# Expert outputs added into a DRAM table of x2 by accumulating scatters, last gate/up weights in two halves, PSUM banks dealt out anew

## What is computed

```python
h2 = _rmsnorm(x, norm2_g) * (1.0 + sc2) + sh2
out = 0
for e in range(32):                      # combine is 0 but for the 2 experts of a token
    hid = silu(h2 @ e_gate[e]) * (h2 @ e_up[e])
    out = out + combine[:, e:e + 1] * (hid @ e_down[e])
x = x + gt2 * out
return _rmsnorm(x, final_norm_g)
```

## Time and profile before

| | |
|---|---|
| median of 3 runs | 1564.2 us (1562.95 to 1564.62) |
| profiled execution, its own time | 1561.74 us |
| its span | 1560.0 us |
| PE busy | 1366.2 us, 88% |
| DVE busy | 598.3 us, 38% |
| ACT busy | 452.2 us, 29% |
| POOL busy | 239.4 us, 15% |
| DMA | 322.78 MB, mean 207 GB/s |
| mean granted PE clock | 0.945 of full speed |

### The profile page before, as it was taken

How to read it: one execution, slowest core, us unless ns; L and a number is a source line. 1 busy time by engine, 2 the same in 40 slices (tenths; PEclk the granted TensorE clock), 3 DMA queues, 4 the chain that set the end, 5 groups by cost and what they waited for, 6 DMA issues and landing times. The chain is left out here.

```text
span 1560.0 us, 30399 instructions
## 1 busy us (share of the span) xinstructions
PE 1366.2 (88%) x13439; PEld 1005.8 (64%) x13439; DVE 598.3 (38%) x1045; ACT 452.2 (29%) x724; POOL 239.4 (15%) x248
## 2 busy tenths in 40 slices
PE   4999999999999996888878999979987888788875
PEld 1788998888998996777767998763333333233322
DVE  3222234452225445555635567542221222112116
ACT  3333243344554543333334543211000000000002
POOL 3000100000112113233400202001111111111116
PEclk9999999999999997999989999969999999999988
DMA  9466442222432120000032264089999999999995
GB/s 335 159 203 206 146 157 68 68 83 89 141 103 68 55 55 23 5 4 4 7 127 68 83 214 155 34 347 403 424 428 426 428 426 427 426 428 426 426 403 197
DMA packets 128554, 322.78 MB, mean 207 GB/s; under 512 B 13849, under 2 KB 99059, under 8 KB 112514
## 3 DMA queue, kind: packets, MB, share of 16 engines
q1 hardware_dynamic: 114224, 289.27, 48.6%
q10 hardware_dynamic: 7522, 15.57, 2.9%
q0 software_dynamic: 6672, 15.95, 2.8%
HBM read 303.25 MB, written 25.11 MB: 210 GB/s over the span
## 5 line engine op out<-in xcount | busy, mean ns | idle before, releaser
L798 PE MATMUL bank<-upper_r 128*128 128x272 f32 x3168 | 419.7, 291 | 5.4 <-DVE upper_r L1037 5.4
L798 PEld LDWEIGHTS bank<-upper_r 128*128 128x128 f32 x3168 | 403.0, 189 | 30.1 <-issue 29.1
L2657 PE MATMUL bank<-upper7b,lower 128*64 128x512 f32 x912 | 254.9, 656 | 74.4 <-issue 73.6
L2657 PEld LDWEIGHTS bank<-upper7b,lower 128*64 128x64 f32 x912 | 84.3, 151 | 208.3 <-issue 206.7
L1014 DVE TENSOR_TENSOR upper_r<-upper,upper_r 128x1024 fp32r<-128x1024 f32 x66 | 82.8, 1255 | 292.5 <-ACT upper_r L571 292.3
L2464 ACT ACTIVATE lower<-bank 128x256 f32<-128x256 f32 x32 | 12.3, 384 | 438.2 <-PE bank L2666 438.2
L3011 DVE COPY lower<-bank 128x512 f32<-128x512 f32 x32 | 22.1, 692 | 278.4 <-PE bank L2657 278.4
L2520 PE MATMUL bank<-upper_r 128*128 128x272 f32 x768 | 103.0, 294 | 2.7 <-DVE upper_r L2906 2.7
L2520 PEld LDWEIGHTS bank<-upper_r 128*128 128x128 f32 x768 | 99.4, 191 | 5.4 <-DVE upper_r L2738 3.1
L2679 PE MATMUL bank<-upper7b,lower 128*64 128x512 f32 x432 | 98.4, 596 | 0.0
L2269 POOL DMA_INDIRECT expert_out<-lower x30 | 44.5, 1484 | 220.8 <-DVE lower L3034 217.2
(11 more groups left out here) (399 smaller groups left out, 1824.0 us busy)
## 6 DMA issues: line engine op xcount, KB each, us to landing
upper7b<-in_expert_w_gate SPq DMA_DIRECT2D x29, 2048.0 KB, 31.3
upper7b<-in_expert_w_up SPq DMA_DIRECT2D x28, 2048.0 KB, 32.9
upper7b<-in_expert_w_down SPq DMA_DIRECT2D x27, 2048.0 KB, 27.9
upper<-in_w_in SPq DMA_DIRECT2D x66, 512.0 KB, 3.8
lower<-in_w_ada SPq DMA_DIRECT2D x23, 1024.0 KB, 5.0
lower<-in_expert_w_down SPq DMA_DIRECT2D x5, 2048.0 KB, 30.0
lower<-in_expert_w_up SPq DMA_DIRECT2D x4, 2048.0 KB, 36.7
lower<-in_expert_w_gate SPq DMA_DIRECT2D x3, 2048.0 KB, 30.7
```

Of the source, the lines that this page charges most:

```text
L798: m = mm(psum[s][:, c, 0:HALF], w_part[s][:, k, :], h_part[:, k, c * HALF:(c + 1) * HALF], start=k == 0 and w_part is w_high and h_part is ...
L2657: m = nc.tensor.matmul(psum[s][64 * b:64 * b + 64, 1, :], x_t[(e // 2) % 2][:, k, s * BLK:(s + 1) * BLK], w[:, k, :], start=k == 0, stop=k ...
```

## The change

1. The table `expert_out` (4T half rows) becomes `expert_sum` (2T half rows, one per token and half). It is not cleared; it starts as x2. The clearing, its row of zeros and the waits for it go.
2. ACT, after each store of h2, also stores that tile of x2 into the table: five more DMAs on its queue.
3. The scatters add to the table (`compute_op=ALU.add`). Since two experts may add to one token's row, scatter e waits on POOL until scatter e-1 has landed, and scatter 0 until x2 is stored.
4. At the end SP reads five tiles of the table into x2 itself. POOL's sums, DVE's `summed`, and POOL's and ACT's share of the final product go; DVE makes all five tiles' outputs. The norm row `fin_g` is loaded ahead of the waits for the scatters instead of behind the reads.
5. Gate and up of expert 31 are loaded as the first half of gate, the first half of up, then the second half of each. PE waits for the second halves before its fifth k.
6. gate/up, turned hidden rows and down get other PSUM banks, and `last_down` for expert 30 runs ahead of down(31) for two tiles instead of one.

```diff
@@ head of the program
-        ys_dram = scratch("expert_out", (T * 4, D // 2))
+        sum_dram = scratch("expert_sum", (T * 2, D // 2))
...
-                pool.dma_start(ys_dram.rearrange("(p n) d -> p n d", p=P),
-                               zero_row[:, 0:512].unsqueeze(1).broadcast_to([P, 17, 512])).then_inc(ys_zero, 16)
...
-                        if g < 2:
-                            act.wait_ge(ys_zero, 16)
-                        else:
+                        if g >= 2:
@@ banks and loads
+        def gu_bank(s):
+            return psum[2 * s][:, 1 - s, :]
+        def hid_bank(s):
+            return psum[1 + s][:, 1, :]
+        def dn_bank(s):
+            return psum[3][:, s, :]
...
+            if kind == "down" or e < NE - 1:
+                sp.dma_start(weights_of(kind, e), source[e]).then_inc(landed[e % 3], 16)
+            else:
+                sp.dma_start(weights_of(kind, e)[:, 0:4], source[e][:, 0:4]).then_inc(landed[e % 3], 16)
+
+        def load_last_half(sp):
+            for kind, source in (("gate", egate), ("up", eup)):
+                sp.dma_start(weights_of(kind, NE - 1)[:, 4:8], source[NE - 1][:, 4:8]).then_inc(wg_rest_in, 16)
@@ SP
                         load_unit(sp, n)
+                        if STREAM[n] == ("up", NE - 1):
+                            load_last_half(sp)
                     sp.wait_ge(gu_mm, r * NE + (NE - 1))
                     sp.sem_inc(held, 1)
-                    sp.wait_ge(dn_mm, r * NE + (NE - 2))
-                    sp.sem_inc(held, 1)
+                    sp.dma_start(fin_g, I["final_norm_g"].partition_broadcast(P)).then_inc(last_rows_in, 16)
                     for s in range(2):
                         sp.wait_ge(y_out9[s], r * (16 * Y_USES[s]) + 16 * Y_USES[s])
                         sp.sem_inc(held, 1)
                     for j, n in TILES:
-                        sp.dma_start(gath[j][0:n].rearrange("t k d -> t (k d)"), ys_v[j * P:j * P + n]
-                                     ).then_inc(gathered[j], 16)
-                    sp.dma_start(fin_g, I["final_norm_g"].partition_broadcast(P)).then_inc(last_rows_in, 16)
+                        sp.dma_start(x2[0:n, j, :], sum_v[j * P:j * P + n]).then_inc(x3_in[j], 16)
@@ POOL
                 def scatter(r, e):
                     pool.wait_ge(y_done, r * NE + (e + 1))
                     pool.sem_inc(held, 1)
-                    pool.indirect_dma_start(ys_dram,
+                    if e:
+                        t = (e - 1) % 2
+                        pool.wait_ge(y_out9[t], r * (16 * Y_USES[t]) + 16 * ((e - 1) // 2 + 1))
+                    else:
+                        pool.wait_ge(x2_kept, r * 80 + 80)
+                    pool.sem_inc(held, 1)
+                    pool.indirect_dma_start(sum_dram,
                                             bass.IndirectOffsetOnAxis(ap=as_u32(y_idx[:, e:e + 1]), axis=0),
-                                            y_blk[e % 2], None, bounds_check=NY - 1, oob_is_err=False
-                                            ).then_inc(y_out9[e % 2], 16)
+                                            y_blk[e % 2], None, bounds_check=NY - 1, oob_is_err=False,
+                                            compute_op=ALU.add).then_inc(y_out9[e % 2], 16)
...
-                    for j, n in TILES:
-                        g = gath[j]
-                        pool.wait_ge(gathered[j], r * 16 + 16)
-                        pool.sem_inc(held, 1)
-                        pool.tensor_tensor(g[0:n, 0, :], g[0:n, 0, :], g[0:n, 1, :], ALU.add).then_inc(g_sum, 1)
...
-                        pool.tensor_tensor(x_fin[j], x2s[i], fin_g, ALU.mult).then_inc(f_pool, 1)
@@ ACT
                     act.dma_start(h2_dram[j * P:j * P + n], h2[i % 2][0:n]).then_inc(h2_kept[i % 2], 16)
+                    act.dma_start(sum_v[j * P:j * P + n], x2[0:n, j, :]).then_inc(x2_kept, 16)
...
-                            nc.scalar.activation(x2s[j - 1], x2[:, j - 1, :], ACT.Copy, scale=sums2[:, j - 1:j]
-                                                 ).then_inc(f_scaled, 1)
@@ PE
                     for k in range(KD):
+                        if e == NE - 1 and k == 4:
+                            pe.wait_ge(wg_rest_in, r * 32 + 32)
+                            pe.sem_inc(held, 1)
...
                         if e == NE - 1:
-                            last_down(r, 0, 0)
+                            for j in range(2):
+                                last_down(r, j, 0)
                         down(r, e)
...
-                    last_down(r, 0, 1)
-                    for j in range(1, 5):
+                    for j in range(2):
+                        last_down(r, j, 1)
+                    for j in range(2, 5):
                         for i in range(NL):
                             last_down(r, j, i)
@@ DVE
-                def summed(r, j):
-                    v.wait_ge(g_sum, r * 6 + (j + 1))
-                    ve.tensor_tensor(x2[:, j, :], x2[:, j, :], gath[j][:, 0, :], ALU.add).then_inc(x2_sum, 1)
...
+                    v.wait_ge(x3_in[j], r * 16 + 16)
...
-                    ve.reciprocal(rs, rs).then_inc(f_done, 1)
-                    if j not in BY_POOL:
-                        v.wait_ge(f_done, r * 8 + NORM_AT[j][0])
-                        ve.scalar_tensor_tensor(out=x_fin[j][0:n], in0=x2[0:n, j, :], scalar=rs, in1=fin_g[0:n],
-                                                op0=ALU.mult, op1=ALU.mult).then_inc(f_done, 1)
+                    ve.reciprocal(rs, rs).then_inc(f_rs, 1)
+                    v.wait_ge(f_rs, r * 5 + (j + 1))
+                    ve.scalar_tensor_tensor(out=x_fin[j][0:n], in0=x2[0:n, j, :], scalar=rs, in1=fin_g[0:n],
+                                            op0=ALU.mult, op1=ALU.mult).then_inc(f_done, 1)
...
+                    for j in range(2):
+                        last_added(r, j)
+                    for j in range(5):
+                        normed(r, j)
+                        if j + 2 < 5:
+                            last_added(r, j + 2)
```

More of the change, by code:

```diff
@@ L184, in build @@
         stage = [S2.take(T) for _ in range(2)]
-        zero_row = Region(chunk_at + R_WORDS + 2 * KD * P).take(D)
         z_at = S2.at
@@ L310, in build @@
         zeroed = sem("zeroed")
-        ys_zero = sem("ys_zero")
         xa_in = sem("xa_in")
@@ L444, in _ @@
                 pool.sem_inc(consts_done, 1)
-                step(pool.memset(zero_row, 0.0))
                 step(pool.memset(alpha_up[0:33, :], 0.0))
@@ L1847, in build @@
         RT_ROWS = RT_CONST + 2 + 24
-        NY = 4 * T
+        NY = 2 * T
         ORDER = [TILES[0], TILES[4], TILES[1], TILES[2], TILES[3]]
@@ L1952, in weights_of @@
             return Region(unit_at(kind, e)).take(*((4, D) if kind == "down" else (KD, FF)))
[L1953 to L1956, removed]
+        fin_g = Region(unit_at("up", NE - 2)).take(D)
+        x_fin = [Region(unit_at("down", NE - 3) + j * D).take(D) for j in range(4)]
+        x_fin.append(Region(unit_at("up", NE - 2) + D).take(D))
         fin_junk = Region(unit_at("gate", NE - 1)).take(D)
@@ L1967, in load_unit @@
             source, landed = {"gate": (egate, wg_in), "up": (eup, wg_in), "down": (edown, wd_in)}[kind]
-            sp.dma_start(weights_of(kind, e), source[e]).then_inc(landed[e % 3], 16)
+            if kind == "down" or e < NE - 1:
[5 more added lines that the diff above has]
+                sp.dma_start(weights_of(kind, NE - 1)[:, 4:8], source[NE - 1][:, 4:8]).then_inc(wg_rest_in, 16)
+        wg_rest_in = sem("wg_rest_in")
+        x2_kept = sem("x2_kept")
         yr_free = sem("yr_free")
@@ L2089, in build @@
         last_mm = sem("last_mm")
-        gathered = [sem(f"gathered{j}") for j, _ in TILES]
-        g_sum = sem("g_sum")
-        x2_sum = sem("x2_sum")
+        x3_in = [sem(f"x3_in{j}") for j, _ in TILES]
         x3_done = sem("x3_done")
@@ L2095, in build @@
         f_std = sem("f_std")
+        f_rs = sem("f_rs")
         f_done = sem("f_done")
-        f_scaled = sem("f_scaled")
-        f_pool = sem("f_pool")
         y_final = sem("y_final")
@@ L2105, in build @@
         Y_USES = [len(range(s, E_LAST, 2)) for s in range(2)]
[L2107 to L2110, removed]
+        sum_v = sum_dram.rearrange("(t b) c -> t (b c)", b=2)
         def first(r):
@@ L2164, in a_round @@
                         sp.sem_inc(held, 1)
-                        sp.wait_ge(blk_zero, r * 1 + 1)
-                        sp.sem_inc(held, 1)
-                        sp.dma_start(ys_dram.rearrange("(p n) d -> p n d", p=P),
-                                     zero_half.unsqueeze(1).broadcast_to([P, 17, 512])).then_inc(y_cleared, 16)
+                        for j, n in TILES:
+                            sp.dma_start(sum_v[j * P:j * P + n], x2[0:n, j, :]).then_inc(x2_kept, 16)
                         for n in range(8):
@@ L2184, in a_round @@
                     for j, n in TILES:
```

(13 more changed lines are left out.)

49 lines of the change are left out of this document (7 added, 42 removed).

## The result

The changed kernel has a median of 1567.88 us (1562.59 to 1575.33, 16 runs) against 1562.11 us of the kernel before (1557.67 to 1564.62, 16 runs). The ratio is 1.0041, with a 95% interval of 1.0028 to 1.0054: slower by 0.4%, on the forecast's side and a little short of its size (+7.9 us, 0.5%; 1567.9 where 1572 was forecast). The profiled execution has a span of 1566.3 us (1560.0 before) and took 1568.12 us.

A forecast was written before the change was run, and what follows sets the result against it. The prediction took the DMA engines to bound the expert stage until the last weights land. Its terms, -7.6 (end) + 1.2 (x2 store) + 14.3 (adding scatters) = +7.9 us, gave 1572 us; range 1555 to 1588, the forecast's own 1567 to 1578.

The forecast's parts named there:

- The stage is bound by the DMA engines: Expert stage: DMA engines, busy all the time at 427 GB/s, set the pace until the last weights land.
- The added row is charged like a read: Adding scatters: fetching destination rows costs as much again as POOL's rows do now, 11.0 us on the mean engine.
- the dearer rival: Adding scatters: the add costs the engine two further reads' worth, +14.3 us more, 1586 us; chance 0.13.
- The slow engines carry 1.3 times the mean: Weight stream: uneven POOL rows, from a lag of some 6 us beside 24 us, raise the add's 11.0 to 14.3 us.
- The x2 store: ACT's queue: one of five stores falls into the weight stream and costs 1.2 us, bounds 0 to 5.
- The wait for the landing costs nothing: POOL in the expert loop: scatter e waiting for scatter e-1 costs 0; later scatters only shift up to some 15 us.
- rival two: Serial scatters become the bound if landing exceeds 15.6 us per expert; at 17.8 it costs 64 us, 1636; chance 0.07.
- The end: After the weights: earlier last matmuls and no POOL sums in DVE's way shorten it by 7.6 us, bounds -7.6 to -4.
- the rival of the idle halves: Last gate and up load: first and second halves land together, so the tail gives only 4.1 us, 1575.6; chance 0.04.
- PE's waits: Profile sign in the expert stage: PE's waits before gate/up grow by some 14 us in all.
- Clearing and its cover: Early in the run: removing the clearing of expert_out is worth 0; without PE's cover its DMA costs at most 15.3 us.
- the free read: Adding scatters: the engine reads and writes at once, add costs 0, queue share stays 4.9%, 1557.8 us; chance 0.32.

The follow-up runs named there:

- add_and_wait: The kernel before with scatters that add into its own cleared table, each also waiting on POOL until the previous one has landed: 1574.14 us, ratio 1.0097.
- add_alone: The kernel before with only its scatters adding into its own cleared table, none waiting for another: 1572.84 us against 1559.73, ratio 1.0084.
- even_before: The kernel before with each expert's few used slots spread over more partitions instead of the block's front: 1552.28 us against 1556.72, ratio 0.9973.
- no_halves: The changed kernel without the split load of the last gate and up weights: 1569.21 us, ratio to the kernel before 1.0082.
- sums_on_pe: The kernel before with split last weights, new PSUM banks, and the two choices summed by PE through identity matmuls instead of by POOL: ratio 1.0031.

## Why the prediction was right, and where it was off

**The stage is bound by the DMA engines.** Right: the loss is in the stream, and no wait on POOL or PE made it (add_and_wait).

**The added row is charged like a read.** Right in kind, and sized too low: the mean engine pays some 13 us (22.5 to 36.0 us from 1040 to 1540), against 11.0 forecast. The packet records of POOL's queue in the two traces show what it pays for. In the kernel before, 2094 are of 4096 bytes; 1088 of them are gathered rows, and 1006 carry two scattered rows each, some 160 ns. Another 32 carry one scattered row (2052 bytes, 85 ns). That makes 10.2 us of 16 engines for the scattered rows. In the changed kernel the same 2044 rows are 2044 records of 2048 bytes and 176 ns, 22.5 us: 2.2 times. Smaller packets, the dearer rival's reason, are the least of it, since a plain row by itself takes 85 ns and not 80; the other 91 ns lie near the 80 that half a gathered row, the same size, takes. The Trainium skill (Collectives: The Full Stack, The bandwidth ceiling: the fold count and why AG ≠ RS ≠ AR) has a collective's reduce in the DMA path at half the speed of a copy for its two source reads. This trace agrees on the price, 176 against 80 to 85 ns for a row; the reads themselves it doesn't count.

**The slow engines carry 1.3 times the mean.** The product of 14.3 us was good (13.7 in add_alone), its factors were not, and that is luck in part. The mean charge came out 2 us higher than forecast, and the stream with the old slots grew by about that mean charge (13.7 us in add_alone), not by 1.3 times it. By the prediction's own step, lag over POOL's time in the stage, the 4.1 us of even_before would give 4.1 / 24 = 0.17 and a factor of 1.17. What the runs do show is the direction: with even slots the same charge of 13.0 us lengthened the stream by only 10.5. Why it is less than the charge stays open.

**The x2 store**: 1.2 forecast, 1.3 by ACT's queue, 1.0 by the stream. The sum for the stream was 15.5, and 15.2 came.

**The wait for the landing costs nothing.** Right (520.3 against 520.4 us), and landings of 10.8 to 12.8 us lie in the forecast span of 10 to 14. The prediction thought that the wait would end before the data was there up to a landing of 11 us; above it, it said, later scatters only shift. That is the case that came, and the serial chain of rival two, with its point at 15.6 us, was some 3 us of landing away.

**The end**: -7.6 forecast, -8.0 measured. PE's wait for down 30 was forecast at 1.8 and is 1.85 us, the products take 1.27 where 1.28 was said. From the last up weights to the end it is 35.3 us (they land at 1531.0) instead of 42.9, shorter by the 7.6 forecast. One step was told wrongly, though the sum was right: it gave the split 3.5 us as if it paid by itself. It pays 3.1 once POOL's sums are gone and 0.3 while they stand. The other share was named about right: 4.9 us without the split (no_halves), where the rival of the idle halves had 4.1.

**PE's waits** were to grow by some 14 us. They grew by 80.4 + 1.9 + 1.3 - 74.9 = 8.7 us (the 1.3 us is the wait for the second halves). PE was also busy 6.2 us longer within the stream (425.8 against 419.6 us). Half of that is slower work: the gate/up matmuls took 258.0 instead of 254.9 us for the same 912, at a mean granted clock of 0.91 instead of 0.92 in the stretch, between its two levels (0.50 as in the row of even_before above, 1.00 as in rows 8). The other half is order: down(30), which ended 2.2 us after the last landing before, now ends ahead of it. The step took PE's work as fixed.

**A sign that failed.** The queue's bytes were to rise like its share. They stayed at 8.66 MB.

**Clearing and its cover.** Not tried alone. The five profiled kernels without the clearing began the stream at 1015.8 to 1027.4 us, the nine with it at 1013.1 to 1021.9, so nothing shows a gain, and one of a few us would not be seen.

**The total** was 7.9 forecast and came as 6.3 us between the profiles, 0.8 of the difference from an earlier start of the stream, which the change does not explain, and as 5.8 between the medians. The 1572 us missed by 4.1: 2.1 of them because the median of the kernel before came down from 1564.2 to 1562.1 with more runs. Against the rivals: the free read would have left the queue at 4.9%; the dearer add would have shown a stream near 536 us; idle halves are excluded by no_halves.

## What to carry to other kernels

When the DMA engines are the bound, count what an edit makes them fetch, not what it stores: the rows read for an accumulate show in no byte count, only in the queue's share of time. The engines that finish last set the pace, so don't let short row lists fill the front partitions; spreading them paid 4.1 us here for one changed pattern. And where two paths end close together, shortening one pays little until the other is gone (the split: 0.3 us, then 3.1), so test such edits in both orders.

## What the runs showed of the hardware

An adding scatter costs the DMA engines about twice a plain one (2.2 times: 22.5 against 10.2 us for 30 scatters; a row of 2 KB takes 176 ns, against 85 alone and 80 in a pair) and lands some 3 us later (12.2 against 8.9 us); the POOL instruction that issues it takes 1971 instead of 1497 ns. The queue's MB do not show the added reads. Eight matmul passes of 512 columns with a 128 x 128 identity took 3.70 us, eight with 64 x 128 of `last_down` 1.99 us. The number of rows is not the reason, since with a 32 x 32 identity eight passes took 3.62 us. Those of `last_down` alternate between partitions 0 to 63 and 64 to 127, the identity's stay on the same ones; that this makes the difference was not tried. The expectation for sums_on_pe had not allowed for it. DVE's product of three operands took 1.28 us with POOL at rest and 1.87 to 3.17 us beside POOL's products in the kernel before.
